# Merge's first phase of a diffusion-transformer step: gate products placed between the sums of h, with three pairs of PSUM banks

## The reference, cut to what matters

```python
sh1, sc1, gt1, sh2, sc2, gt2 = ada_mod(cond, w_ada, b_ada)
h = rmsnorm(x, g_mix) * (1 + sc1) + sh1
gq, gk, gv, gr, zf, zb, nq, nk, nv, m_gla, m_na = split_in(h @ w_in)
...
b_gla = (rmsnorm(o_gla, g_gla).reshape(B, T, GLA_V) * jax.nn.silu(gr)) @ w_gla_o
...
b_na = o_na.reshape(B, T, NA_W) @ w_na_o
mix = (jax.nn.sigmoid(m_gla) * b_gla + jax.nn.sigmoid(m_na) * b_na) @ w_out
x = x + gt1 * mix
h2 = rmsnorm(x, g_ffn) * (1 + sc2) + sh2
x = x + gt2 * conv_ffn(h2, w_up, w_conv, b_conv, w_down)
```

## Time and profile before

| | us |
|---|---|
| median of three runs | 1010.01 (1007.35 to 1010.16) |
| profiled execution, its own time | 1008.67 |
| its span, first to last instruction | 1006.9 |
| PE busy | 977.9 (97%) |
| DVE, ACT, POOL busy | 607.1, 448.7, 513.3 |
| stage of the gate products after the attention, 383.97 to 419.25 | 35.28 |
| pairs, groups and half of the NA products, 419.25 to 495.65 | 76.40 |
| the other NA products to the end of Out's first chunk, 495.65 to 519.65 | 24.00 |

### The profile page before, as it was taken

How to read it: one execution, slowest core, us unless ns; L and a number is a source line. 1 busy time by engine, 2 the same in 40 slices (tenths; PEclk the granted TensorE clock), 3 DMA queues, 4 the chain that set the end, 5 groups by cost and what they waited for, 6 DMA issues and landing times.

```text
span 1006.9 us, 18181 instructions
## 1 busy us (share of the span) xinstructions
PE 977.9 (97%) x7139; PEld 908.8 (90%) x7139; DVE 607.1 (60%) x1091; ACT 448.7 (45%) x696; POOL 513.3 (51%) x361
## 2 busy tenths in 40 slices
PE   4999999999999998999999999999999999999998
PEld 3999999999788888899988899999999999788886
DVE  7507358964365658643684899777777778813002
ACT  4243264442676666333342455555555556611110
POOL 1475731222342323675470467888888886533331
PEclk9999999999999999999999999999999999999999
DMA  9978222213011112587662122222222231322231
GB/s 339 309 85 104 63 63 64 63 45 84 12 23 42 43 43 76 160 274 266 225 230 83 42 85 83 86 85 85 85 85 85 85 95 53 105 91 77 88 127 56
DMA packets 132076, 105.51 MB, mean 105 GB/s; under 512 B 6902, under 2 KB 112283, under 8 KB 131739
## 3 DMA queue, kind: packets, MB, share of 16 engines
q1 hardware_dynamic: 127112, 97.32, 32.4%
q0 software_dynamic: 1568, 3.15, 2.2%
q10 hardware_dynamic: 3315, 3.94, 1.1%
HBM read 99.91 MB, written 3.42 MB: 103 GB/s over the span
## 4 chain that ended last, share of the span: by engine, by line
PE 83%; DVE 8%; issue 3%; POOL 2%; DMA 2%; ACT 1%; SPq 0%; DVEq 0%; POOLq 0%; ACTq 0%
PE PJ L882 8%; PE PJ L887 7%; PE PJ L883 7%; PE PA L1470 6%; PE PA L1472 6%; PE PA L1471 6%; PE PA L1363 3%; PE PA L1364 3%; PE PA L1365 3%; PE PJ L1363 3%; PE PJ L1364 3%; PE PJ L1365 3%; PE PJ L1189 2%; PE PA L1206 2%; PE PA L1020 2%
## 5 line engine op out<-in xcount | busy, mean ns | idle before, releaser
L668 POOL TENSOR_TENSOR wlo<-wraw,whi 128x1024 fp32r<-128x1024 f32 x54 | 139.7, 2588 | 272.0 <-ACT whi L1523 184.8
L882 PE MATMUL PJ<-h_hi,whi 128*128 128x320 f32 x512 | 158.0, 316 | 0.4 <-ACT qk_rs L1678 0.4
L883 PE MATMUL PJ<-h_lo,whi 128*128 128x320 f32 x512 | 154.3, 309 | 0.0
L887 PE MATMUL PJ<-h_hi,wlo 128*128 128x320 f32 x512 | 116.6, 309 | 0.0
L882 PEld LDWEIGHTS PJ<-h_hi,whi 128*128 128x128 f32 x512 | 96.4, 188 | 3.2 <-issue 1.4
L883 PEld LDWEIGHTS PJ<-h_lo,whi 128*128 128x128 f32 x512 | 96.5, 189 | 0.0
L887 PEld LDWEIGHTS PJ<-h_hi,wlo 128*128 128x128 f32 x512 | 85.6, 188 | 0.0
L1523 ACT ACTIVATE whi<-wraw 128x1024 fp32r<-128x1024 f32 x39 | 40.9, 1050 | 57.8 <-PE PJ L887 51.6
L2021 ACT ACTIVATE whi<-wraw 128x1024 fp32r<-128x1024 f32 x21 | 22.3, 1060 | 99.7 <-PE PA L1365 51.6
L839 POOL TENSOR_TENSOR behind<-behind_val,behind 128x512 fp32r<-128x512 f32 x40 | 52.1, 1302 | 19.0 <-ACT behind L2000 19.0
L1472 PE MATMUL PA<-h_hi,behind 128*128 128x320 f32 x192 | 59.3, 309 | 0.0
(11 more groups left out here) (541 smaller groups left out, 3112.6 us busy)
## 6 DMA issues: line engine op xcount, KB each, us to landing
wraw<-in_w_in_dram SPq DMA_DIRECT2D x74, 256.0 KB, 3.1
ada_rest<-in_w_ada_dram SPq DMA_DIRECT2D x32, 512.0 KB, 5.6
wraw<-in_w_up_dram SPq DMA_DIRECT2D x48, 256.0 KB, 3.8
wraw<-in_w_down_dram SPq DMA_DIRECT2D x42, 256.0 KB, 3.0
raw_even<-in_w_up_dram SPq DMA_DIRECT2D x40, 256.0 KB, 3.7
ada<-in_w_ada_dram SPq DMA_DIRECT2D x8, 1024.0 KB, 10.5
out_dram<-x ACTq DMA_DIRECT2D x10, 256.0 KB, 2.0
x_rows<-in_x_sample_dram SPq DMA_DIRECT2D x2, 1024.0 KB, 6.6
```

The lines of the kernel that those rows point to most:

```text
L668: pool.tensor_tensor(wlo[:, slot, 0:k, :], wraw[:, slot, 0:k, :], whi[:, slot, 0:k, :].bitcast(F32), ALU.subtract).then_inc(lo_done, 1)
L882: pe.matmul(out, whi[:, slot, w0 + k, :], hi(k)[:, tok], start=start and k == k0, stop=False)
L883: pe.matmul(out, whi[:, slot, w0 + k, :], lo(k)[:, tok], start=False, stop=False)
L887: mm = pe.matmul(out, wlo[:, slot, w0 + k, :], hi(k)[:, tok], start=False, stop=stop and k == k1 - 1)
```

## The change

- A product writes one of three bank pairs by `j % 3`: PJ's two pairs and PA's banks 0 and 1. From product 3 on it waits for gate j-3; product 2 waits for none.
- On DVE the gate multiplications are put between the sums: gate 0 behind the first sum, 1 behind the second, 2, 3 and 4 behind differences two to four, 5 to 7 between the low halves. S2 waits for gate 5, since it lies in PA's bank 1. The last low half of the attention output (`pair_low(3)`) and the memset of `rows_all` go behind these, ahead of the pair loop.
- On ACT three sigmoids come first, then chunk 3 (ahead of the first difference's high half), and chunk 4 ahead of the fourth's.
- On SP pair 1 and then the other parts of group 0 go ahead of the wait for `rows_zero`; the load of group 7 goes ahead of a chunk of Out.
- On PE and DVE the groups move by some products: 0 from behind P5 to behind P4 of pair 0; 1 to behind P6 of pair 1; 2 and 3 to pair 2 behind P5 and P2; 4 to behind P3 of pair 3; 5, 6 and 7 to behind NA products 1, 4 and 7. The last `columns` goes into Out's first chunk.

The diff, cut:

```diff
@@ -389,6 +389,10 @@
+        def gate_banks(j):
+            return halves(PA, 0) if j % 3 == 2 else halves(PJ, j % 3)
@@ -548,6 +552,13 @@
+            sp.wait_ge(lo_done, C_GO + 3)
+            m_pair(1, ("A11", "A12"))
+            sp.wait_ge(lo_done, C_GO + 4)
+            m_pair(1, ("A21", "A22"))
+            sp.wait_ge(tm_lo, 4)
+            for a in (2, 3):
+                ada_rest_piece(a, ADA_FIRST * P)
@@ -564,13 +575,6 @@
-            sp.wait_ge(lo_done, C_GO + 3)
-            m_pair(1, ("A11", "A12"))
-            sp.wait_ge(tm_lo, 4)
-            for a in (2, 3):
-                ada_rest_piece(a, ADA_FIRST * P)
-            sp.wait_ge(lo_done, C_GO + 4)
-            m_pair(1, ("A21", "A22"))
@@ -617,8 +621,8 @@
+                    rest_load(7)
...
-                    rest_load(7)
@@ -1263,14 +1267,15 @@
+                banks = gate_banks(j) if done is bg_ps else halves(PJ, j % 2)
...
-                        out = PJ[:, (j % 2 * 2 + b) * BANK:(j % 2 * 2 + b) * BANK + HALF]
+                        out = banks[:, b, :]
...
-                        out = PJ[:, (j % 2 * 2 + b) * BANK:(j % 2 * 2 + b) * BANK + HALF]
+                        out = banks[:, b, :]
@@ -1291,8 +1296,8 @@
-                    else:
-                        pe.wait_ge(t1_set, j - 1)
+                    elif j >= 3:
+                        pe.wait_ge(t1_set, j - 2)
@@ -1328,22 +1333,22 @@
+                mixed("P5", p, 1)
+                if p == 2:
+                    rest(2)
+                mixed("P6", p, 2)
...
-                mixed("P5", p, 1)
+                mixed("P7", p, 3)
+                mixed("P4", p, 4)
...
-                mixed("P6", p, 2)
+                mixed("P3", p)
...
-                mixed("P7", p, 3)
-                mixed("P4", p, 4)
+                mixed("P2", p)
...
-                mixed("P3", p)
-                if p == 1:
-                    rest(2)
-                mixed("P2", p)
@@ -1353,9 +1358,8 @@
-                if j in (0, 3, 6):
+                if j in (1, 4, 7):
...
-            columns(NK - 1)
@@ -1377,11 +1381,10 @@
-                if q != 3 and len(tiles) == 2:
+                if q != 3 and tiles == (3, 4):
...
-            pe.wait_ge(ada2_rows, NK)
@@ -1389,7 +1392,12 @@
-                out_chunk(n, (0, 1, 2))
+                if n == 0:
+                    out_chunk(n, (0, 1))
+                    columns(NK - 1)
+                    out_chunk(n, (2,))
+                else:
+                    out_chunk(n, (0, 1, 2))
@@ -1820,17 +1828,16 @@
-            gate_sigmoid(0)
-            gate_sigmoid(1)
+            for j in range(3):
+                gate_sigmoid(j)
+            go_high(2)
...
-            go_high(2)
-            gate_sigmoid(2)
+            gate_sigmoid(3)
...
-            gate_sigmoid(3)
+            gate_sigmoid(4)
...
+            go_high(3)
...
-            gate_sigmoid(4)
-            go_high(3)
@@ -2379,7 +2386,7 @@
-                dve.tensor_tensor(by_half(sg[:, j, :]), halves(PJ, j % 2), by_half(sg[:, j, :]), ALU.mult).then_inc(t1_set, 1)
+                dve.tensor_tensor(by_half(sg[:, j, :]), gate_banks(j), by_half(sg[:, j, :]), ALU.mult).then_inc(t1_set, 1)
@@ -2389,16 +2396,17 @@
-                gated_gla(0)
+                    gated_gla(k // 4)
...
-                gated_gla(1)
+                gated_gla(2)
...
+                gated_gla(3)
...
-                gated_gla(2)
+                gated_gla(4)
@@ -2441,13 +2449,8 @@
-            dve.wait_ge(pt_ps, 20)
-            dve.wait_ge(pv_ps, 20)
-            dve.wait_ge(sc_mx, 40)
-            dve.wait_ge(on_lo, 4)
-            dve.memset(rows_all[:, :, :], 0.0).then_inc(rows_zero, 1)
+                    break
@@ -2465,6 +2468,8 @@
+                else:
+                    dve.wait_ge(t1_set, 6)
@@ -2516,39 +2521,43 @@
-            gated_gla(3)
...
+            gated_gla(5)
+            m_second_sum(0)
...
-            gated_gla(4)
-            m_second_sum(0)
+            gated_gla(6)
+            m_second_low(0)
...
-            gated_gla(5)
-            m_second_low(0)
+            gated_gla(7)
...
-            gated_gla(6)
-            gated_gla(7)
+            pair_low(3)
+            dve.wait_ge(pt_ps, 20)
+            dve.wait_ge(on_lo, 4)
+            dve.memset(rows_all[:, :, :], 0.0).then_inc(rows_zero, 1)
...
-                if p < 2:
-                    rest_kept(p)
+                if p == 2:
+                    rest_kept(2)
...
-                if p == 3:
-                    rest_kept(4)
+                if p == 1:
+                    rest_kept(1)
...
+                if p == 0:
+                    rest_kept(0)
+                m_sum("C12", p, "P3", tmp[:, :], a[:, far])
+                if p == 3:
+                    rest_kept(4)
+                m_fourth_sum(p + 1)
+                m_sum("C11", p, "P2", a[:, near], a[:, near])
...
-                m_sum("C12", p, "P3", tmp[:, :], a[:, far])
-                if p == 1:
-                    rest_kept(2)
-                m_fourth_sum(p + 1)
-                m_sum("C11", p, "P2", a[:, near], a[:, near])
@@ -2562,9 +2571,11 @@
+                if j == NK - 1:
+                    rest_kept(j)
...
-                if j in (0, 3, 6):
+                if j in (1, 4):
```

## The result

| | us |
|---|---|
| median after (5 runs, 1001.38 to 1002.93) | 1002.21 |
| median before beside it (5 runs, 1007.26 to 1010.16) | 1008.77 |
| ratio | 0.9934, 95% interval 0.9919 to 0.9949 |
| profiled execution after, and its span | 1002.16, 1000.4 |

What follows compares the result with a forecast made beforehand. The prediction took TensorE, busy 97% of the span, as the bound, gaining only where it waits. 5.76 - 0.3 + 0 = 5.45 us, from a base of 1009.65, gave 1004.2 us; range for 8 in 10: 1000.2 to 1008.6.

Steps and rivals of the forecast that it cites:

- The bound and the place: PE, product 1 to first Merge product: 6.49 us lost around waits for gates, of which 5.76 us would be gained.
- The walk of the queues: Gate stage, DVE, ACT and POOL stepped through: products 2 to 5 and 7 wait for nothing, product 6 waits 0.73 us.
- The turn rule: DVE instructions with two SBUF inputs and POOL instructions reading SBUF take turns; the second to issue blocks; PSUM-reading gate multiplications are exempt.
- Behind the products: DVE's late low halves and memset: last low half at 418.6, memset 421.4 to 422.3, slacks of 0.6 to 2 us.
- The 0.3 us set aside for P6 and group 0: Merge of pair 0: allowance for P6 waiting 0.9 us after a lost turn and group 0 waiting 0 to 1.0 us.
- Group 0 and SP's queue: Group 0 behind P4: data landing at 422.9, needed at 423.4; pair 1 going ahead clears SP; pair 2 costs nothing.
- The rival "SP's queue": Chance 0.05, slower: a memset some 13 us late holds pair 2's load behind rows_zero on SP; 1013 us and more.
- Other groups: The modulation's groups elsewhere: moved without any wait, cost 0, bounds 0 and 0.5 us.
- Group 7 and the last columns: Up to 1.4 us gained, against a 1.5 us wait at the last transposition; taken as 0, bounds 0.4 loss, 1.4 gain.
- The sum: Whole kernel: 5.76 - 0.3 + 0 = 5.45 us gained, forecast 1004.2 us from a base of 1009.65.
- Everything closes: Rival, chance 0.13: the fourth chunk and DVE's copy arrive in time; 6.49 + 1.4 us gained, 1001.8 us.

Runs made afterwards that it cites:

- chunk 3 later: The changed kernel with ACT's conversion of weight chunk 3 back behind the first difference's high half; its one execution took 1006.52 us.
- group 0 back: The changed kernel with the modulation's group 0 back behind P5 of pair 0 on PE, three products earlier; 1008.97 us, ratio 1.0 to before.
- SP's order back: The changed kernel with pair 1's loads and group 0's last two parts again behind SP's wait for rows_zero; 1009.53 us, ratio 1.0011 to before.
- banks alone: The kernel before with three bank pairs and the wait for gate j-3, DVE's order kept except S2 behind gate 5; 1010.27 us, ratio 1.002.

## Why the prediction was right, point by point

**The bound and the place.** Right: of the edited stages only the one between product 1 and P1 gains, 5.93 us where 5.76 were forecast and 6.49 were there.

**The walk of the queues.** Right to about 0.4 us, once all is shifted by the 0.83 us by which product 0 starts later. DVE and POOL in order of time, after (first difference, second, fourth, the first two low halves, S2's low half, the last two low halves, memset; POOL's third chunk, S1, fourth chunk, S3, S3's low half):

```profile
394.24 3.35 DVE L2401 TENSOR_TENSOR M_val<-hf 128x1280 f32<-128x1280 f32 x1
397.62 2.47 DVE L2403 TENSOR_TENSOR M_val<-hf,M_val 128x1280 f32<-128x1280 f32 x1
402.88 1.48 DVE L2408 TENSOR_TENSOR hf<-hf,M_val 128x1280 f32<-128x1280 f32 x1
405.01 3.30 DVE L2459 TENSOR_TENSOR M_lo<-M_val,M_hi 128x1280 fp32r<-128x1280 f32 x1
409.95 2.58 DVE L2459 TENSOR_TENSOR M_lo<-M_val,M_hi 128x1280 fp32r<-128x1280 f32 x1
413.19 0.68 DVE L2484 TENSOR_TENSOR m_ahead<-PA,m_ahead 128x512 fp32r<-128x512 f32 x1
413.79 1.48 DVE L2459 TENSOR_TENSOR M_lo<-M_val,M_hi 128x1280 fp32r<-128x1280 f32 x1
415.92 1.85 DVE L2461 TENSOR_TENSOR h_lo<-hf,h_hi 128x1280 fp32r<-128x1280 f32 x1
419.96 0.91 DVE L2537 MEMSET rows_all<- 128x1024 f32 x1 [0.35 <-DVE ona_lo L2371]
...
393.82 2.42 POOL L672 TENSOR_TENSOR wlo<-wraw,whi 128x1024 fp32r<-128x1024 f32 x1 [6.39 <-ACT whi L1531]
396.20 2.55 POOL L782 TENSOR_TENSOR m_s<-m_raw 128x512 f32<-128x512 f32 x1
404.56 2.41 POOL L672 TENSOR_TENSOR wlo<-wraw,whi 128x1024 fp32r<-128x1024 f32 x1 [5.82 <-ACT whi L1531]
411.15 2.55 POOL L782 TENSOR_TENSOR behind_val<-m_raw 128x512 f32<-128x512 f32 x1
415.08 1.35 POOL L768 TENSOR_TENSOR behind<-behind_val,behind 128x512 fp32r<-128x512 f32 x1 [1.38 <-ACT behind L1799]
```

The walk had the third chunk at 393.0 (393.83 with the shift; measured 393.82), the first difference done at 396.8 (397.63; 397.59), the second at 399.5 (400.33; 400.09) and the fourth chunk from 404.0 to 406.4 (407.23; 406.97). Product 6 started 0.48 us late instead of 0.73. Both are counted as the walk counts: the last two matmuls of product 5 begin at 406.26, two steps of 0.147 later PE is ready, at 406.55 as walked; the 0.31 in the row is counted from the modelled end of the last matmul. The chunk came 0.26 earlier, and the walk's own times give 0.68 (406.4 - 405.72) where 0.73 was written. With the slower restart the stage lost 0.56 of the 6.49 us. The turn rule carried this part: the first difference took 3.35 us beside POOL and 1.48 without it, in the run with chunk 3 later. (In the rule's own check 400.08 - 397.73 + 1.38 is 3.73, not 3.70; nothing hangs on it.) The Trainium skill, "SBUF — State Buffer", section "Who interferes with whom", has such a DVE instruction, when it issues second, fully blocked by POOL; these two rows agree.

**Behind the products.** The walk was too late by 1.7 us, on the safe side: `h_lo` ended at 417.77 where 418.6 + 0.83 was walked, the memset began at 419.96 instead of 422.2. The low halves themselves took about what was walked: 3.30 and 2.58 us in turns with POOL, the third its own 1.48 with POOL idle until 415.08, the last 1.85. The largest single error, 0.6 us, is S2's low half. The walk let it wait for POOL's S3, yet it reads one operand from PSUM, as the gate multiplications do, which by the walk's own rule take no part; it ran in 0.68 us at 413.19, inside S3 (411.15 to 413.70). The other 1.1 us are small leads, the fourth chunk's 0.26 among them. So the parts of group 0 left at 417.80, landed some 4.3 us later and were there before the group began at 423.06. The 0.3 us set aside for P6 and group 0 measured 0.

**Group 0 and SP's queue.** No wait was the likeliest case, and none came; but what this hides was not priced. The prediction named the landing time and the cleared queue. It did not say that the old place of group 0 would give back 5.1 us and the old order of SP 7.3. The rival "SP's queue" looked at the memset and pair 2, which stayed clear; the queue's real victim is group 0's own last parts, and the new order keeps them out of that trap.

**Other groups.** No wait: 76.41 against 76.40 us.

**Group 7 and the last columns.** The mechanism was right: group 7's wait went, and the transposition waits for `rest_rows`. The term was mis-sized: 1.18 us instead of 1.5, counted from the step at which PE was ready (the row's 1.02 is counted from the modelled end). The net, forecast as 0 with 0.4 of loss as one bound, was a loss of 0.12.

**The sum.** 5.45 us forecast, 5.8 measured in the stages: the missing part is the 0.3 for group 0 and 0.17 of product 6, less 0.12 at the end. The time came out 2 us below 1004.2 mostly for another reason: before ran at 1008.77 beside it, where I had put the base at 1009.65. That is 0.9 us, 0.35 more is the sum, and 0.36 is the wait at 609, which the forecast did not have. The remaining 0.4 us is less than what two profiles of one kernel differ by. That the base was too high and the gain too small did not cancel: both put the forecast on the slow side, and the range took it in. "Everything closes" (1001.8) lies nearer to the measured time, but not to what happened: neither of its two waits had closed.

## What to carry to other kernels

When an engine in the middle serves two customers from one queue, write its order so that each result comes just ahead of the instruction that needs it; more buffers without that only let the wait collect at the next shared buffer (0.96 us from the banks behind the right order, slower behind the old one). When work on the bounding engine moves up, ask of each transfer behind it what cover it had: here 5.8 us of gain stood or fell with the place of one group and with the order of one queue. A small wait that is left can be cheap to close by moving its producer up or its consumer behind independent work: two moves of a few lines took 1.45 us more.

## What the hardware showed beyond that

A wait on TensorE can cost more than its length. The granted clock fell from 1.00 (2.4 GHz) to 0.50 (1.2 GHz) behind waits of 1.97, 3.35 (2.72 and 0.63), 4.85 and 5.1 us, and stayed there for some 3 to 3.5 us (one profile each). Taking the wait away from the whole loss leaves that part, some tenths for the restart behind a wait included (before, four waits of 5.5 us cost 6.49): group 0 back, 5.14 - 3.35 = 1.8 us; SP's order back, 7.3 - 5.3 = 2.0; chunk 3 later, 3.2 - 1.66 more of wait = 1.5; banks alone, 5.25 - 3.61 = 1.6. Yet in the kernel before, waits of up to 2.07 us in the same stage left the clock at 1.00. Nor does it fall in every execution: a stretch of 3.4 us at 0.50 makes a mean of 0.998 over the span, and one of the ten executions of "group 0 back" ran at a mean of 1.000. No trace of it was kept, but it was the fastest, 1005.82 us, where the others took 1007.72 to 1010.21 at 0.993 to 0.998. Why the clock fell behind 1.97 us in the one kernel and not behind 2.07 in the other stays open; the length of the wait alone does not decide it.
